# A two-block transformer kernel: input transposed on the host and normalised after the first projections, gate matmuls in three passes, and weight halves made by casting and accumulating transfers

## The chip, the cores and the metric

One core of one Trainium2 chip runs the whole program. The metric is the time of one execution on the device in microseconds (us), taken as the median over runs; the profile is of one execution.

## The reference

Two blocks work on 256 tokens of width 1024, all in float32. Cut to what matters:

```python
h = rms_norm(x, norm1_g)
proj = h @ w_in
(rx, rgate, q, kc, vc, ks, vs, kw, vw, nsa_g, mg_rnn, mg_attn) = jnp.split(proj, splits, axis=-1)
hr = rg_lru(causal_dwconv(rx, ...), rg_w_a, rg_b_a, rg_w_x, rg_b_x, lru_lambda)   # gates: block-diagonal products
y_rnn = (hr * gelu(rgate)) @ w_rnn_out
o = nsa(q, kc, vc, ks, vs, kw, vw, nsa_g, ...)   # keys and queries are RMS-normalised per head
x = x + (sigmoid(mg_rnn) * y_rnn + sigmoid(mg_attn) * (o @ w_attn_out)) @ w_out
up = causal_dwconv(rms_norm(x, norm2_g) @ w_up, ...)
x = x + (gelu(gate) * val) @ w_down
# second block: mixer of attention and gated MLP, layer norms, SwiGLU
```

## The kernel before

**Precision.** Nearly every product is made of three passes in fp32r, a rounded 32-bit form. A weight chunk w is split into a high part WH = round(w), which ScalarE (ACT) writes by a copy (L630), and a low part WL = w − WH, which VectorE (DVE) writes (L1075). Activations are split likewise (BH and BL, CH and CL, AH and AL, kept side by side in BHL, CHL, AHL). TensorE (PE) adds high×high, low×high and high×low in PSUM. `f_tile` is the form with weights stationary: for each of two column halves, 16 matmuls on WH (L1736, L1737), a wait for the low part, then 8 on WL (L1741).

**Chunks.** The weights come as a stream of 135 chunks, most of 128×2048 floats (1 MB), in one order that every engine's program follows. SyncE's queue (SP) loads chunk after chunk into RAW slots (two through most of the program); a slot is loaded anew when its last chunk's low part has been written. WH and WL have three slots; chunk c's are free when PE is through chunk c−3. In iteration c of its loop ACT (and DVE behind it) does `split(c + 2)`, reads the results of chunk c out of PSUM (`side(c)`), and does the attention work that falls into this window (`window(c - W0)`). Each engine works strictly in its written order; semaphores do the rest.

The chunks up to the end of the attention stage, by number: 0 to 3 kv (keys and values), 4 and 5 cmp, 6 to 9 q, 10 and 11 w1 (fp32, not split), 12 to 14 rnn, 15 mg0, 16 ri0, 17 and 18 rnn, 19 mg1, 20 ri1, 21 mg2, 22 and 23 rnn, 24 mg3, 25 ri2, 26 mg4, 27 and 28 rnn, 29 mg5, 30 ri3, 31 and 32 rnn, 33 mg6, 34 mg7, 35 ri4, 36 to 39 ao. An rnn chunk projects the recurrent branch, mg a merge gate, ri the recurrent gates of one group of two tiles (three in ri1), ao the attention's output.

**The opening.** x is loaded in token order; ACT and DVE sum squares, POOL (GpSimd) takes the root; PE runs 14 fill matmuls meanwhile (L2334), then transposes the scaled first token tile (L2340) and the second against a scaled diagonal (L2345). ACT and DVE evict these with the gain as BH and BL, and kv0 and kv1 start, 48 matmuls of 512 columns (L2018, L2021, L2024).

**The attention stage.** It begins in chunk 17 and has 12 units spread over windows. PE computes scores (L1859); DVE masks and reduces (L1096, L1098); ACT takes exponentials (L651); DVE scales; PE transposes (L1870); ACT copies half of the transposed tile PT (L663), DVE the other half (L1120); PE multiplies with the values (L1893). The ri chunks use fp32 matmuls straight from the convolved XC (L2070), with 42-row cross blocks where a block straddles two tiles (L2078, L2080); ACT reads them with tanh (L807, L808). Two PSUM banks serve cmp, rnn, mg and ri in turn: matmul group m waits until group m−2 has been read. One to three chunks after an ri chunk ACT's window holds its exponential and tanh, and the "root stage": square root (L726) and gelu (L728), each with a table load.

Of the kernel before, what the change touches and what calls it, by code (L numbers as in the profile page):

```python
# [23 lines left out]
ACT = mybir.ActivationFunctionType  # L24
# [3 lines left out]
P = 128  # L28
TOK = 256
# [41 lines left out]
def gate_cols(g):  # L71

    return RG_TILES[g] * RP + HB
# [17 lines left out]
def chunk_list():  # L91

    out = [("kv", i, CHUNK, True) for i in range(4)]
    out += [("cmp", i, CHUNK, True) for i in range(2)]
    out += [("q", i, CHUNK, True) for i in range(4)]
# [3 lines left out]
    for g in range(NG):  # L99
# [4 lines left out]
        out += [("ri", g, 2 * gate_cols(g), False)]  # L104
# [12 lines left out]
def ffn_order(up, n, down, lag=5):  # L117

    out, d = [], 0
    for i in range(n):  # L120
        out.append((up, i, CHUNK, True))
        if i >= 2 * d + lag:
# [13 lines left out]
               max(RNN_NO[i] for i in range(RG_AT[g], RG_AT[g + 1])) + 1 for g in range(NG)]  # L136
SPLIT_NO = [sum(1 for x in CHUNKS[:c] if x[3]) for c in range(NCH)]
PLAIN = [c for c in range(NCH) if not CHUNKS[c][3]]

# [4 lines left out]
def arrival_slots():  # L144

    last, uses, out = [None] * (NRAW + 3), [0] * (NRAW + 3), {}
    for c, (kind, i, _, is_split) in enumerate(CHUNKS):
# [7 lines left out]
        last[slot] = SPLIT_NO[c]  # L155
# [23 lines left out]
SPLIT_AHEAD = AT[("ri", 0)]  # L179

# [65 lines left out]
def two_block_program(nc, A_w, A_x, A_cols, A_consts, A_g1, A_g2, A_og, A_gln, A_ln1, A_ln2, A_ws, A_out):  # L246
    ctx = ExitStack()
    with ctx:
# [45 lines left out]
        def const(name):  # L294
# [69 lines left out]
        G1 = put("G1", [P, KD], at=pr + 43008)  # L364
# [58 lines left out]
        w_hi, w_lo, chunk_done, tile0_done, ri_part, y_gain, x_again, const_in, g1_in = (sem(n) for n in (  # L423
            "w_hi", "w_lo", "chunk_done", "tile0_done", "ri_part", "y_gain", "x_again", "const_in", "g1_in"))
        warm_ready, rows_in, w0_half, dg_ready, w0_in, ws_in, out_done, act_own, dve_own = (sem(n) for n in (
            "warm_ready", "rows_in", "w0_half", "dg_ready", "w0_in", "ws_in", "out_done", "act_own", "dve_own"))
        pool_own, x_sq, x_rstd, w0_lo, xt_done, xt_hi, xt_lo, k_sq, k_ss = (sem(n) for n in (
            "pool_own", "x_sq", "x_rstd", "w0_lo", "xt_done", "xt_hi", "xt_lo", "k_sq", "k_ss"))
        k_rstd, kn_ready, kt_done, kt_copied, gk_ready, mb_act, mb_dve, gate_tanh = (sem(n) for n in (
            "k_rstd", "kn_ready", "kt_done", "kt_copied", "gk_ready", "mb_act", "mb_dve", "gate_tanh"))  # L430
        gate_ready, q_sq, q_ss, rq_ready, lam_exp, lam_abs, c4_ready = (sem(n) for n in (
            "gate_ready", "q_sq", "q_ss", "rq_ready", "lam_exp", "lam_abs", "c4_ready"))
# [6 lines left out]
        pt0_copied, pt1_copied, pv_done, o_hi, o_lo, rnn_g, la_ready = (sem(n) for n in (  # L439
            "pt0_copied", "pt1_copied", "pv_done", "o_hi", "o_lo", "rnn_g", "la_ready"))  # L440
# [14 lines left out]
        y_mean, y_std, eps_ready, x0_low, y_ln, xt4_done, xt4_hi, xt4_lo, up2_silu, up2_prod = (sem(n) for n in (  # L455
            "y_mean", "y_std", "eps_ready", "x0_low", "y_ln", "xt4_done", "xt4_hi", "xt4_lo", "up2_silu", "up2_prod"))
        up2_hi, up2_lo, z_gain, wt_ready, rnn_in, xw_ready, gate_t_done, x_sq2 = (sem(n) for n in (
            "up2_hi", "up2_lo", "z_gain", "wt_ready", "rnn_in", "xw_ready", "gate_t_done", "x_sq2"))
        half_copied, halves_summed = sem("half_copied"), sem("halves_summed")
# [2066 lines left out]
```

## Time and profile before

| | us |
|---|---|
| median of 3 runs | 811.58 (811.54 to 811.63) |
| the profiled execution's own time | 811.55 |
| its span, first to last instruction | 809.8 |
| PE busy | 799.9 |
| DVE busy | 599.0 |
| ACT busy | 486.6 |
| POOL busy | 27.1 |

The span is what the profile covers; 1.75 us of the execution's time lie around it. Busy time says how long an engine had an instruction in work, with overlapping matmuls counted once; the waits say who held whom. The mean granted clock of TensorE is 0.997.

### The profile page before, as it was taken

How to read it: one execution, taken by the hardware profiler on the slowest of the kernel's cores; microseconds unless marked ns; L12 is line 12 of the kernel's file. 1: busy time of each engine (PE TensorE's matmuls, PEld its weight loads, DVE VectorE, ACT ScalarE, POOL GpSimd, SP SyncE). 2: the span in 40 equal slices, each digit the busy share in tenths (PEclk: the TensorE clock that was granted, in tenths of full speed). 3: DMA queues.
4: the chain of work that ended last, by engine and by line, in shares of the span. 5: the costliest groups of instructions: out<-in, count | busy, mean ns of one | idle time of the engine just before them, and what ended most of it. 6: DMA issues, size and time to landing. Idle time of an engine off the chain costs nothing.

```text
span 809.8 us, 11913 instructions
## 1 busy us (share of the span) xinstructions
PE 799.9 (99%) x4813; PEld 694.6 (86%) x4813; DVE 599.0 (74%) x773; ACT 486.6 (60%) x738; POOL 27.1 (3%) x38
## 2 busy tenths in 40 slices
PE   9999999999999999999999999999999999999996
PEld 8889998888888888988888888888888888888885
DVE  6774698998958986897878678877777665655556
ACT  6555598877767454665666566546755654544552
POOL 1102000000000000000000000020110000000000
PEclk9999999999999999999999999999999999999998
DMA  8446433342434774456555555664453655465431
GB/s 338 160 159 251 169 126 105 118 155 70 154 119 159 251 266 156 156 197 219 161 204 182 197 193 183 253 240 142 144 197 123 211 198 201 170 220 190 162 151 52
DMA packets 22630, 143.79 MB, mean 178 GB/s; under 512 B 2608, under 2 KB 3248, under 8 KB 8240
## 3 DMA queue, kind: packets, MB, share of 16 engines
q1 hardware_dynamic: 20880, 137.72, 48.0%
q10 hardware_dynamic: 1696, 5.31, 1.9%
q8 instruction: 38, 0.62, 0.3%
q14 instruction: 16, 0.13, 0.1%
HBM read 141.97 MB, written 1.05 MB: 177 GB/s over the span
## 4 chain that ended last, share of the span: by engine, by line
PE 92%; ACT 3%; DVE 3%; issue 1%; DMA 1%; DVEq 0%; SPq 0%; ACTq 0%
PE PS L1749 19%; PE PS L1753 10%; PE PS L1802 10%; PE PS L1803 10%; PE PS L1806 10%; PE PS L1736 5%; PE PS L1737 4%; PE PS L1741 4%; PE PS L2120 2%; PE PS L1765 2%; PE PS L2099 2%; PE PS L1859 1%; PE PS L2124 1%; PE PS L1893 1%; PE PS L1870 1%; PE PS L1773 1%
## 5 line engine op out<-in xcount | busy, mean ns | idle before, releaser
L1075 DVE TENSOR_TENSOR WL<-RAW,WH 128x2048 fp32r<-128x2048 f32 (+2 forms) x127 | 284.6, 2242 | 32.3 <-ACT WH L630 32.1
L630 ACT ACTIVATE WH<-RAW 128x2048 fp32r<-128x2048 f32 (+2 forms) x127 | 238.1, 1877 | 51.3 <-PE PS L1806 26.4
L1491 DVE TENSOR_TENSOR HLS<-PS,HLS 128x512 f32<-128x512 f32 x46 | 31.7, 689 | 92.7 <-ACT HLS L978 92.7
L1749 PE MATMUL PS<-CHL,WH 128*128 128x512 f32 x352 | 87.9, 392 | 0.0
L1736 PE MATMUL PS<-BHL,WH 128*126 128x256 f32 (+1 forms) x336 | 83.8, 287 | 0.0
L978 ACT ACTIVATE HLS<-PS 128x512 f32<-128x512 f32 x46 | 27.4, 595 | 90.8 <-PE PS L1753 86.4
L1737 PE MATMUL PS<-BHL,WH 128*126 128x256 f32 (+1 forms) x336 | 81.8, 282 | 0.0
L1749 PE MATMUL PS<-BHL,WH 128*128 128x512 f32 x320 | 79.9, 392 | 0.0
L1749 PEld LDWEIGHTS PS<-CHL,WH 128*128 128x128 f32 x352 | 63.9, 189 | 11.8
L1803 PE MATMUL PS<-WH,AHL 128*128 128x512 f32 x176 | 68.8, 391 | 0.0
L1802 PE MATMUL PS<-WH,AHL 128*128 128x512 f32 x176 | 68.7, 390 | 0.0
L1736 PEld LDWEIGHTS PS<-BHL,WH 128*126 128x126 f32 (+1 forms) x336 | 63.4, 189 | 4.6 <-issue 4.0
L1749 PEld LDWEIGHTS PS<-BHL,WH 128*128 128x128 f32 x320 | 58.1, 189 | 10.7
L1737 PEld LDWEIGHTS PS<-BHL,WH 128*126 128x126 f32 (+1 forms) x336 | 63.5, 189 | 0.0
L1802 PE MATMUL PS<-WH,BHL 128*128 128x512 f32 x160 | 63.2, 395 | 0.0
L1803 PE MATMUL PS<-WH,BHL 128*128 128x512 f32 x160 | 62.4, 390 | 0.0
L1806 PE MATMUL PS<-WL,AHL 128*128 128x512 f32 x176 | 54.4, 390 | 0.0
L1753 PEld LDWEIGHTS PS<-CHL,WL 128*128 128x128 f32 x352 | 48.0, 190 | 3.4
L1753 PE MATMUL PS<-CHL,WL 128*128 128x256 f32 x352 | 49.1, 282 | 0.0
L1741 PE MATMUL PS<-BHL,WL 128*126 128x256 f32 (+1 forms) x336 | 46.7, 281 | 0.0
L1753 PEld LDWEIGHTS PS<-BHL,WL 128*128 128x128 f32 x320 | 43.7, 190 | 3.1
L1502 DVE SCALAR_TENSOR_TENSOR CG<-HLS,CV,CG 128x255 f32<-128x255 f32 (+1 forms) x96 | 44.1, 481 | 1.7
(313 smaller groups left out, 1312.3 us busy)
## 6 DMA issues: line engine op xcount, KB each, us to landing
RAW<-in_w_stream SPq DMA_DIRECT2D x108, 1024.0 KB, 4.9
RAW<-in_w_stream SPq DMA_DIRECT2D x11, 1008.0 KB, 4.8
RAW<-in_w_stream SPq DMA_DIRECT2D x8, 704.0 KB, 4.7
WF<-in_w_stream SPq DMA_DIRECT2D x2, 1024.0 KB, 5.2
LN<-in_ln ACTq DMA_DIRECT2D x2, 1024.0 KB, 5.1
WF<-in_w_stream SPq DMA_DIRECT2D x4, 294.0 KB, 3.6
X<-in_x SPq DMA_DIRECT2D x2, 512.0 KB, 4.2
RAW<-in_w_stream SPq DMA_DIRECT2D x2, 512.0 KB, 6.6
```

Of the source, the lines that this page charges most:

```text
L630: eng.activation(WH[:, c % NSLOT, 0:CHUNKS[c][2]], raw(c), ACT.Copy).then_inc(w_hi, 1)
L1075: eng.tensor_tensor(WL[:, c % NSLOT, 0:CHUNKS[c][2]], raw(c), f32(WH[:, c % NSLOT, 0:CHUNKS[c][2]]), ALU.subtract).then_inc(w_lo, 1)
L1491: eng.tensor_tensor(HLS[:, n % 4, :, :], PS[:, bank:bank + 2, 0:TOK], HLS[:, n % 4, :, :], ALU.add)\
L1502: ins = eng.scalar_tensor_tensor(o, HLS[:, i % 4, v, 0:TOK - s], col("fw", (2 - s) * 2 * N_UP + f), o, ALU.mult, ALU.add)
L1736: eng.matmul(out, wh, H[0:parts, k, :], start=(k == 0), stop=False)
L1737: eng.matmul(out, wh, L[0:parts, k, :], start=False, stop=False)
L1741: last = eng.matmul(out, wl, H[0:parts, k, :], start=False, stop=(k == nk - 1))
L1749: eng.matmul(PS[:, bank, :], wh, HL[:, k, :, :].rearrange("p a t -> p (a t)"), start=(k == 0), stop=False)
L1753: last = eng.matmul(PS[:, bank, 0:TOK], wl, HL[:, k, 0, :], start=False, stop=(k == KD - 1))
L1802: eng.matmul(out, H[:, k, tile], wh, start=(start and n == 0), stop=False)
L1803: eng.matmul(out, L[:, k, tile], wh, start=False, stop=False)
L1806: last = eng.matmul(out, H[:, k, tile], WL[:, s, lo_:lo_ + cols], start=False, stop=(stop and n == len(ks) - 1))
```

## The change

- **Opening.** The host also passes x transposed, with the gain in front (`xt`, tile XTG with XT inside it). CH and CL are XT times the gain, split, without the row's root. kv0 to kv3 and q are computed from CH and CL, eight pieces of kv0 and kv1 at a time (`first_high`, `first_low`), and the row scale rsx is applied where V, the keys' and the queries' squares and roots are made. x itself is loaded behind kv3. After kv3 PE spreads the row scales by two fp32 matmuls, DVE scales XT (`input_normed`), and ACT and DVE split it into BH and BL for the rest. q0 and q1 come before cmp. 11 fills stand in place of 14.
- **Gates.** The ri chunks are split as others are; ACT rounds XC into AH (`rg_round`), DVE writes the remainder into AL, and each product has three passes. A cross block is 106 columns wide with zeros, to start at the bank's partition 0.
- **Casting transfers.** For the 16 split chunks from 17 to 39 that are not mg (`CAST`), WH is written by a transfer on POOL's queue, which reads the chunk again and rounds it. RAW is still loaded for the low part, which DVE now writes in iteration c−1.
- **Accumulating transfers.** For mg1 to mg7 (`ADDED`), ACT still writes WH. At the end of iteration c−2 it writes −w, rounded, into WL (`negated`), and a transfer on POOL's queue adds the chunk from memory in place. The RAW slot is free after the negation.
- **PT.** ACT copies both halves at once.
- Some semaphores are joined, without another order.

```diff
+ADDED = [AT[("mg", i)] for i in range(1, 8)]
+CAST = [c for c in range(AT[("ri", 0)] + 1, AT[("ao", 3)] + 1) if CHUNKS[c][3] and c not in ADDED]
...
+            for c in range(NCH):
+                if c + 2 in CAST:
+                    s, n = (c + 2) % NSLOT, CAST.index(c + 2)
+                    source = A_w[OFFS[c + 2]:OFFS[c + 3]].rearrange("(p n) -> p n", p=P)
+                    eng.wait_ge(chunk_done, c)
+                    if n >= 2:
+                        eng.wait_ge(wh_in[n % 2], 16 * (n // 2))
+                    eng.dma_start(WH[:, s, 0:CHUNKS[c + 2][2]], source).then_inc(wh_in[n % 2], 16)
+                if c + 2 in ADDED:
+                    s, n = (c + 2) % NSLOT, ADDED.index(c + 2)
+                    source = A_w[OFFS[c + 2]:OFFS[c + 3]].rearrange("(p n) -> p n", p=P)
+                    eng.wait_ge(neg_ready, n + 1)
+                    if n:
+                        eng.wait_ge(wl_in, 16 * n)
+                    eng.dma_start(WL[:, s, 0:CHUNKS[c + 2][2]], source, accum_op=ALU.add).then_inc(wl_in, 16)
...
+            def negated(c):
+                eng.activation(WL[:, c % NSLOT, 0:CHUNKS[c][2]], raw(c), ACT.Copy, scale=-1.0).then_inc(neg_ready, 1)
...
+            def rg_round(i):
+                G, t = RG_OF[i]
+                eng.wait_ge(mb_dve, RNN_NO[i] + 1)
+                eng.activation(AH[0:RP, i, :], XC[:, G % 2, t, :], ACT.Copy).then_inc(xc_hi, 1)
...
                 if c >= W0:
                     window(c - W0)
+                if c + 2 in ADDED:
+                    negated(c + 2)
...
-                if c and CHUNKS[c - 1][0] == "ri" and c - 1 != SPLIT_AHEAD or c == UNIT_FIRST:
+                if c + 1 in CAST:
                     split(c + 1)
+                if c + 1 < NCH and CHUNKS[c + 1][0] == "ri":
+                    s, n = (c + 1) % NSLOT, CHUNKS[c + 1][2]
+                    wait_both(eng, c + 1)
+                    eng.tensor_tensor(WL[:, s, 0:n], raw(c + 1), f32(WH[:, s, 0:n]), ALU.subtract).then_inc(rg_low, 1)
...
                 if CHUNKS[c][3]:
                     slot, before, _ = ARRIVAL[c]
                     if before is not None:
-                        eng.wait_ge(w_lo, before + 1)
+                        if before in ADDED:
+                            eng.wait_ge(neg_ready, ADDED.index(before) + 1)
+                        elif CHUNKS[before][0] == "ri":
+                            eng.wait_ge(rg_low, RG_LOW_NO[CHUNKS[before][:2]])
+                        else:
+                            eng.wait_ge(w_lo, LOW_NO[before] + 1)
...
-            def f_tile(out, c, col0, m, H, L, nk=KD, parts=P):
+            def f_tile(out, c, col0, m, H, L, nk=KD, parts=P, first_use=False):
...
                     eng.matmul(out, wh, H[0:parts, k, :], start=(k == 0), stop=False)
                     eng.matmul(out, wh, L[0:parts, k, :], start=False, stop=False)
-                eng.wait_ge(w_lo, SPLIT_NO[c] + 1)
+                wait_low(eng, c)
...
                         for which in range(2):
-                            last = eng.matmul(PS[0:RP, banks[t], 256 * which:256 * which + 256],
-                                              w[0:RP, which, RP * t:RP * t + RP], XC[:, i % 2, t, :], start=(which == 0),
+                            rows = wh[0:RP, which, RP * t:RP * t + RP]
+                            eng.matmul(outs[which], rows, AH[0:RP, k, :], start=(which == 0), stop=False, skip_group_check=True)
+                            eng.matmul(outs[which], rows, AL[0:RP, k, :], start=False, stop=False, skip_group_check=True)
+                        for which in range(2):
+                            last = eng.matmul(outs[which], wl[0:RP, which, RP * t:RP * t + RP], AH[0:RP, k, :], start=False,
                                               stop=(t == 2), skip_group_check=True)
...
-            for _ in range(14):
+            for _ in range(11):
                 eng.matmul(PS[:, 4, 0:P], WARM[:, :], WARM[:, :], start=True, stop=True)
-            eng.wait_ge(g1_in, 32)
-            for kp in range(4):
-                eng.wait_ge((x0_low, dg_ready)[kp // 2], 1)
...
```

How instructions moved, at three places. First PE at the start of the program. Before (WARM is the fill tile, CN holds the identity, XN the scaled x, DG the diagonal):

```order
L2334 MATMUL PS<-WARM 128x128 x13
L2340 MATMUL PS<-CN,XN 128x128 [waits x0_low,g1_in]
L2340 MATMUL PS<-CN,XN 128x128
L2340 MATMUL PS<-CN,XN 128x128 [waits x0_low]
L2340 MATMUL PS<-CN,XN 128x128
L2340 MATMUL PS<-CN,XN 128x128 [waits dg_ready]
...
L2345 MATMUL PS<-DG,X_115 128x128 [waits dg_ready]
L2345 MATMUL PS<-DG,X_115 128x128 x7
L2018 MATMUL PS<-WH,BHL 128x512 [waits xt_hi,w0_half]
L2018 MATMUL PS<-WH,BHL 128x512 x3
```

Now:

```order
L2504 MATMUL PS<-WARM 128x128 x10
L2183 MATMUL PS<-WH,CHL 128x512 [waits xt_ready,w_part_hi]
L2183 MATMUL PS<-WH,CHL 128x512
L2186 MATMUL PS<-WL,CHL 128x512 [waits w_part_lo]
L2186 MATMUL PS<-WL,CHL 128x512
L2189 MATMUL PS<-WH,CHL 128x512 [waits xt_lo]
L2189 MATMUL PS<-WH,CHL 128x512
```

The transposes are gone, and the first weight matmuls stand right behind the fills, two for each pass instead of four.

Second ACT in iteration 17, the one in which chunk 19 (mg1) is prepared; its exponential and tanh (AA, TR), then the root stage of group 0. Before:

```order
L718 ACTIVATE AA<-TR 126x512 [waits la_ready]
L719 ACTIVATE TR<-TR 126x512 [waits act_own]
L721 ACTIVATE XC<-AA 126x512 [waits ix_ready]
L726 ACT_TABLE_LOAD
L726 ACTIVATE XC<-TR 126x512 [waits w_ready]
L728 ACT_TABLE_LOAD
L728 ACTIVATE RGT<-RGT 126x512 [waits rnn_g]
L794 ACTIVATE XC<-PS,CV 126x256 [waits chunk_done]
```

Now:

```order
L808 ACTIVATE AA<-TR 126x512 [waits la_ready]
L809 ACTIVATE TR<-TR 126x512 [waits act_own]
L811 ACTIVATE XC<-AA 126x512 [waits ix_ready]
L816 ACT_TABLE_LOAD
L816 ACTIVATE XC<-TR 126x512 [waits w_ready]
L818 ACT_TABLE_LOAD
L818 ACTIVATE RGT<-RGT 126x512 [waits rnn_g]
L715 ACTIVATE WL<-RAW 128x2048
L747 ACTIVATE AHL<-XC 126x256 [waits mb_dve]
L892 ACTIVATE XC<-PS,CV 126x256 [waits chunk_done]
```

The negation (WL<-RAW) and the rounding of the convolved tile stand between the root stage and the next chunk's results.

Third POOL's queue, behind the compressed keys' root (crs). Before:

```order
L575 TENSOR_SCALAR tmp<-css 64x1 [waits kc_sq]
L576 TENSOR_TENSOR crs<-tmp,half 64x1 [waits pool_own]
L597 TENSOR_TENSOR rs_87<-ss1s,half 128x1 [waits x1_ss] x2
L601 TENSOR_TENSOR RQK<-RT 128x512 [waits rope_parts] x2
L604 AFFINE_SELECT WS<-WS 128x1024 [waits ws_in]
```

Now (17 more transfers follow in the same manner until rs_87):

```order
L634 TENSOR_SCALAR tmp<-css 64x1 [waits kc_sq]
L635 TENSOR_TENSOR crs<-tmp,half 64x1 [waits pool_own]
L669 DMA WH<-in_w_stream 128x2016 [waits chunk_done] x2
L676 DMA WL<-in_w_stream 128x2048 [waits neg_ready]
L669 DMA WH<-in_w_stream 128x968 [waits wh_in0,chunk_done]
L676 DMA WL<-in_w_stream 128x2048 [waits wl_in,neg_ready]
L669 DMA WH<-in_w_stream 128x2016 [waits wh_in1,chunk_done]
```

The queue that did nothing in the attention stage now issues 23 transfers in it, each casting one behind the accumulating ones of earlier chunks.

## Rows read from the trace of the kernel before

**Rows 1.** The page: span, and busy us (share of the span) with instructions.
```profile
span 809.8 us, 11913 instructions
...
PE 799.9 (99%) x4813; PEld 694.6 (86%) x4813; DVE 599.0 (74%) x773; ACT 486.6 (60%) x738; POOL 27.1 (3%) x38
```
**Rows 2.** Waits of PE: engine, line, who was waited for; us, times, longest.
```profile
PE PS L1870 <- DVE PT L1120: 0.8, 1, 0.8
```
**Rows 3.** Timeline of the opening: start us, us, engine, line, operation.
```profile
1.10 6.08 PE L2334 MATMUL PS<-WARM 128*128 128x128 f32 x28 [1.10 <-DVE WARM L1641]
...
4.56 0.63 ACT L1024 ACTIVATE XN<-X 128x512 f32<-128x512 f32 x1 [1.57 <-DMA X<-in_x]
...
7.42 1.06 PE L2340 MATMUL PS<-CN,XN 128*128 128x128 f32 x8 [0.24 <-ACT XN L1027]
...
10.12 1.18 PE L2018 MATMUL PS<-WH,BHL 128*128 128x512 f32 x4
...
11.64 1.92 ACT L630 ACTIVATE WH<-RAW 128x2048 fp32r<-128x2048 f32 x1
...
21.14 0.39 PE L1802 MATMUL PS<-WH,BHL 128*128 128x512 f32 x1
```
**Rows 4.** Busy us by stretch: PE, PEld, DVE, ACT, POOL, PEclk, DMA share, GB/s.
```profile
10.10:21.30 11.20, 11.20 (x52) 9.28 (x51) 10.60 (x19) 9.10 (x12) 0.00 (x0) 1.00 0.89 352
98.60:137.10 38.50, 38.44 (x297) 33.32 (x294) 33.98 (x47) 34.20 (x70) 0.00 (x0) 1.00 0.36 124
```
**Rows 5.** DMA issues: count, KB each, median us from issue to landing.
```profile
RAW<-in_w_stream SPq DMA_DIRECT2D x108, 1024.0 KB, 4.9
...
CN<-in_consts SPq DMA_DIRECT2D x1, 229.0 KB, 8.8
```
**Rows 6.** PE timeline of chunk 16 (ri0) and the scores behind it.
```profile
98.89 1.89 PE L2070 MATMUL PS<-XC,WF 126*126 126x256 f32 x8
100.71 0.41 PE L2078 MATMUL PS<-XC,WF 42*42 42x256 f32 x1
...
101.70 1.14 PE L1859 MATMUL PS<-KT,QT 64*128 64x256 f32 x8
```
**Rows 7.** ACT timeline, iterations 17 to 20.
```profile
105.22 1.90 ACT L630 ACTIVATE WH<-RAW 128x2048 fp32r<-128x2048 f32 x1
...
115.59 0.63 ACT L728 ACTIVATE RGT<-RGT 126x512 f32<-126x512 f32 x1
...
122.85 0.62 ACT L663 ACTIVATE PT<-PS 128x512 f32<-128x512 f32 x1
123.57 0.47 ACT L807 ACTIVATE TR<-PS,hba 126x256 f32<-126x256 f32 x1
```
**Rows 8.** PE timeline: first low pass of chunk 19 (mg1); chunk 20 (ri1).
```profile
117.80 1.12 PE L1741 MATMUL PS<-BHL,WL 128*128 128x256 f32 x8
...
122.51 3.08 PE L2070 MATMUL PS<-XC,WF 126*126 126x256 f32 x12
```
**Rows 9.** DVE timeline in window 4.
```profile
101.53 2.25 DVE L1075 TENSOR_TENSOR WL<-RAW,WH 128x2016 fp32r<-128x2016 f32 x1
```
**Rows 10.** ACT's root stages and PE's low passes of chunks 24, 29 and 34.
```profile
148.68 0.85 ACT L728 ACTIVATE RGT<-RGT 126x768 f32<-126x768 f32 x1
...
152.61 1.12 PE L1741 MATMUL PS<-BHL,WL 128*128 128x256 f32 x8
...
188.10 0.63 ACT L728 ACTIVATE RGT<-RGT 126x512 f32<-126x512 f32 x1
...
195.22 1.12 PE L1741 MATMUL PS<-BHL,WL 128*128 128x256 f32 x8
...
227.70 0.63 ACT L728 ACTIVATE RGT<-RGT 126x512 f32<-126x512 f32 x1
...
232.58 1.12 PE L1741 MATMUL PS<-BHL,WL 128*128 128x256 f32 x8
```
**Rows 11.** Busy us by stretch at the end, columns as in rows 4.
```profile
802.70:805.40 2.70, 0.00 (x0) 0.00 (x0) 2.59 (x5) 1.53 (x3) 0.00 (x0) 1.00 0.13 48
805.60:809.80 4.20, 0.00 (x0) 0.00 (x0) 1.68 (x5) 0.00 (x0) 0.00 (x0) 0.50 0.50 187
```

More of the change, by code:

```diff
@@ L71, in gate_cols @@
 def gate_cols(g):
[L73 removed]
+    return RG_TILES[g] * RP + 64 + HB
 def rnn_rows(g):
@@ L154, in arrival_slots @@
         out[c] = (slot, last[slot], uses[slot])
-        last[slot] = SPLIT_NO[c]
+        last[slot] = c
         uses[slot] += 1
@@ L1026, in _ @@
-            eng.wait_ge(x_rstd, 1)
-            eng.activation(XN[:, 0, 0:512], X0[:, 0, 0:512], ACT.Copy, scale=rsx[:, 0:1]).then_inc(x0_low, 1)
-            eng.wait_ge(g1_in, 32)
-            for kp, ready in enumerate((w0_half, w_hi)):
-                eng.wait_ge((w0_in, raw_in[ARRIVAL[0][0]])[kp], 16)
-                part = slice(CHUNK // 2 * kp, CHUNK // 2 * kp + CHUNK // 2)
-                eng.activation(WH[:, 0, part], raw(0)[:, part], ACT.Copy).then_inc(ready, 1)
-                gained_hi(kp)
@@ L1233, in side @@
-                if kind == "kv" and i == 0:
+                if kind == "kv" and i == 1:
+                    key_sums(0)
+                if kind == "q" and i == 0:
                     eng.wait_ge(const_in, 32)
@@ L1691, in _ @@
                     rg_squares(rg_group(c - W0, RG_SQUARES))
-                if CHUNKS[c][:2] not in SUMS_FIRST and kind != "ri" and c != W0 and c + 1 != UNIT_FIRST or c == SPLIT_AHEAD:
+                if c == 1:
+                    x_squares()
+                if c == 3:
+                    input_normed()
+                if kind == "w1" and i == 0:
+                    queries_normed(1, 0)
+                if c == 4:
+                    key_sums(1)
+                    for kp in range(4):
+                        eng.wait_ge(xt_hi, KD - 1 + kp + 1)
+                        pair = slice(2 * kp, 2 * kp + 2)
+                        eng.tensor_tensor(BL[:, pair, :], XT[:, pair, :], f32(BH[:, pair, :]), ALU.subtract).then_inc(xt_lo, 1)
+                if c == 5:
+                    query_sums(0)
+                    keys_normed(0)
+                if CHUNKS[c][:2] not in SUMS_FIRST and c + 2 not in CAST and c != W0:
                     split(c + 2)
@@ L1704, in _ @@
                     rg_scan(G)
+                if c == 1:
+                    roots_diagonal()
+                if c == 5:
+                    keys_normed(1)
+                if kind == "w1" and i == 0:
+                    queries_normed(1, 1)
+                if c == W0:
+                    decay_rates()
                 side(c)
```

526 lines of the change are left out of this document (306 added, 220 removed).

## Prediction

> **What bounds it now.** I read the page first: TensorE (PE) is busy 799.9 us of an 809.8 us span [rows 1]. Overlapping matmuls flatter that number, so I asked who TensorE waits for. After the opening one wait is listed, 0.8 us for a copy on VectorE [rows 2]. In the attention stage the matmuls start at their usual cadence with no hole: PE's instruction stream is the time, and whatever stops it is paid in full. The exception is the opening: fill matmuls start at 1.10, transposes of the normalised input at 7.42, and the first weight matmul at 10.12 [rows 3]. The span is 809.8, the execution's time 811.55, 0.03 below the median, 811.58; I sum against 811.55.
>
> **The opening.** The three steps before the matmuls (squares, scaled copies, transposes) leave the path: 24 transposing instructions, 7.42 to 10.12. The remaining limit is the 11 fills. 28 starts took 6.08 less a tail [rows 3], so 22 end near 1.10 + 22 × 0.21 = 5.8. The first pieces (256 KB of weights and 266 KB of input) equal the 512 KB that the first squaring waited for until 4.56 [rows 3]; with a copy of a quarter chunk (a quarter of 1.92 us) they are ready at about 5.1. The same 48 matmuls ran from 10.12 to 21.14, 0.227 each; from 5.8 they end at 16.7: −4.4. Behind them stands the supply. Chunks kv0, kv1, kv2 and the transposed input are 4.2 MB; at 352 GB/s [rows 4] from about 3.1 (the 512 KB transfer's landing less its 1.5 us) the last lands at 15.1; its high copy takes 1.92 [rows 3] to 17.0 (+0.3), its low part another 2.25 [rows 9] to 19.3, where PE wants it eight matmuls after 17.0, at 18.8 (+0.5). The matmuls that spread the row scales, two fp32 ones of two instructions at some 0.11, add 0.4. Net **−3.2**, from −4.4 (supply no limit) to 0 (the queue that now also carries the input and x feeds PE late).
>
> **The gates.** Before, a group of two 126-row tiles issues 8 instructions in 1.89, 0.22 each, then four pairs of 42-row matmuls from 100.71 to 101.70, 0.25 a pair [rows 6]; over five groups that is 44 and 20. Now 66 matmuls in three passes at 0.12 (eight low-part matmuls take 1.12 with their tail [rows 8]) replace the 44: 7.8 for 9.5. The cross blocks become 30 pairs. If a pair still runs together, they cost 3.5 for 4.5; if one after the other, 7.1. I take together, since K = 64 matmuls on separate row halves do so before (8 in 1.14 [rows 6]). Net **−2.7**, up to +0.9. The work added on ACT and DVE (rounding and remainder of 11 tiles of 256 columns, each no longer than the 512-column copy of 0.62 [rows 7]) lies beside matmuls; without that cover its 22 pieces would cost up to 14.
>
> **Relief of ACT and DVE.** 16 high copies of up to 1.9 leave ACT for transfers on POOL's queue; DVE loses seven low parts of 2.25 [rows 9], and its half of twelve PT copies goes to ACT. PE waited for them only 0.8 [rows 2]: **−0.8**. The sixteen casting transfers have a whole chunk or more of PE time, so I cost them at nothing; they double the reading of those chunks.
>
> **What replaces the low part of a merge gate.** The new chain is: ACT writes −w (one copy, 1.9), POOL's queue wakes, 1 MB is read and added in place, and only then may PE start the low pass. ACT's copy stands at the end of iteration c−2, behind everything there. The chunks, by iteration:
> - mg1 (chunk 19, ACT iteration 17). Before, ACT runs without a hole from 105.22 (the high copy of mg1) to 116.22 (the gelu of group 0): 26 rows, none with an idle time ahead, the first and last in [rows 7]. The negation follows. PE starts mg1's low pass at 117.80 [rows 8]. Moreover the high copy of mg1 needs its RAW slot, whose last reader is now DVE's low part of chunk 17. That part stands one chunk later than before, where DVE ran another at 101.53 to 103.78 [rows 9]; with 4.9 us of transfer [rows 5] the data lands at 108.7, 3.5 after 105.22. SP's queue and the exponentials of unit 0 stand behind it. The negation so ends at 116.2 + 3.5 + 1.9 = 121.6.
> - ri1 (chunk 20). The negation of mg2 is put before the gates' tanh. PE's third tile waits for that tanh: two tiles done at 122.7 + 1.4 = 124.1, while ACT comes free of its PT copy at 123.5 [rows 7], now 0.4 later since it does both halves (an estimate from its 0.62 for one), then 1.9 of negation and two tanh of 0.47: 126.7. **+2.6**. The transfer of mg2 then lies beside it.
> - mg3, mg5, mg7 (chunks 24, 29, 34). Their negation stands behind the same root stage, which ends at 149.53, 188.73 and 228.33; the low passes start at 152.61, 195.22 and 232.58 [rows 10]. With transfer time T the stalls are T − 1.2, T − 4.6, T − 2.3.
> - mg4 and mg6 have no root stage ahead; nothing.
>
> No row shows an accumulating transfer. The nearest is a plain 1 MB load, 4.9 us, as the lower end; the upper is 8.8, a transfer that lands behind others [rows 5]. In two of three cases another 1 MB load starts with it, since the negation frees a RAW slot. I take **T = 5.5**, near the plain row, because the DMA engines are busy only 0.36 of the time here [rows 4]. Then: mg1 121.6 + 5.5 − 117.8 = **+9.3**, ri1 +2.6, mg3 **+4.3**, mg5 **+0.9**, mg7 **+3.2**.
>
> The Trainium skill (DMA: Bandwidth & Descriptors, "Anatomy of one DMA — SWDGE (gpsimd) path") gives for a transfer issued by GpSimd about 2.0 us plus bytes at 436 GB/s, some 4.4 us for this megabyte. By that estimate the stalls would be 1.1 shorter each; no run here shows one, and the sum keeps to the row of 4.9 and above.
>
> **The clock.** The fills start every 0.21 us, the 128-column transposes after them (8 in 1.06) about every 0.11 [rows 3]: PE is at 1.2 GHz at first and at 2.4 after 6 us of work. After PE's last matmul (before 802.7) the granted clock is 0.50 from 805.6 on [rows 11]. So a stall of some 3 us or more may be followed by half rate, which costs at most half of 6 us each. I take **+1** over all, since two stalls are that long. The skill (TensorE: Matmul & The Clock Gate, "HAM oscillation — how this bites in real kernels") tells the same of kernels that wait for DMA; what it adds is the rival below.
>
> **Sum.** −3.2 − 2.7 − 0.8 = −6.7; + 9.3 + 2.6 + 4.3 + 0.9 + 3.2 + 1.0 = +21.3. 811.55 + 14.6 = **826**.
>
> **Rivals.**
> - *The negations run ahead, and only the gains are left*: 811.55 − 6.7 = **805**. For it: ACT is free of 16 copies. Against it: those copies don't stand between 105.22 and 116.22, nor in the root stages, and even a transfer of no length leaves mg1 at 118.1 for 117.8. It needs mg1's negation to end before 112.3 (with T = 5.5). 12 in 100.
> - *Short waits*: raw data of mg1 in time and T = 4.9. Then mg1 116.2 + 1.9 + 4.9 − 117.8 = 5.2, ri1 2.6, mg3 3.7, mg5 0.3, mg7 2.6: 14.4 − 6.7, **819**. 22 in 100.
> - *The clock falls at each long stall* (mg1, mg3, mg7): 3 × 3 in place of 1: **834**. 12 in 100.
> - *The accumulating transfer is slow*, 8.8: each of four stalls 3.3 longer: **839** and more. 3 in 100.
> - *Even*: gains and stalls of 7 cancel, **811.5**, if mg1 alone stalls. 5 in 100.
> - My forecast: 46 in 100.
>
> **Numbers.** Within 0.2% (1.6 us) I call it no change, about what three runs of this kernel can tell. Slower holds 83 in 100, the same 5, faster 12. The range takes in the forecast, the short waits and the clock: 813 to 840.
>
> **What would show it.** After: the first weight matmul near 5.8 and the 48 done near 17; gate groups about 0.5 us shorter. In the waits of PE, the DMA of WL as releaser in mg1's low pass, of 6 us or more, and again in mg3 and mg7; ACT's TI ahead of the third tile of ri1. The casting transfers should appear in no wait. I am wrong in size if T is far from 5.5, wrong in kind if PE waits for no WL transfer, and wrong in the opening if PE then waits for high copies of chunks kv2 or later by more than 1 us.

## The result and the profile after

The changed kernel takes **865.25 us** (median of 4 runs, 864.2 to 867.74) against 811.56 for the kernel before beside it: 1.0667 of its time, interval 1.0652 to 1.0681. Slower, as forecast, but by 53.7 us where 14.6 were forecast; the range ended at 840.

The page of the changed kernel, answering to [rows 1], [rows 5] and, by PEclk, [rows 4]:

```profile
span 866.0 us, 12016 instructions
...
PE 811.4 (94%) x4829; PEld 707.0 (82%) x4829; DVE 592.0 (68%) x788; ACT 490.5 (57%) x752; POOL 54.1 (6%) x69
...
PEclk9999968968999899999999999999999999999998
...
RAW<-in_w_stream SPq DMA_DIRECT2D x107, 1024.0 KB, 5.0
...
WH<-in_w_stream POOLq DMA_DIRECT2D x8, 1008.0 KB, 12.2
WL<-in_w_stream POOLq DMA_DIRECT2D x7, 1024.0 KB, 10.4
...
WH<-in_w_stream POOLq DMA_DIRECT2D x4, 1024.0 KB, 7.0
```

PE, busy 99% of its span before, is now busy 94%, and its clock is cut in slices of the attention stage; the last slice reads 8 as it did before. The accumulating transfer takes 10.4 us from issue to landing, not 5.5. The waits of PE, answering to [rows 2] (engine, line, releaser; us, times, longest):

```profile
PE PS L1906 <- DMA WL<-in_w_stream: 38.5, 7, 10.4
...
PE PS L1901 <- DVE XC L1422: 2.8, 1, 2.8
```

All seven merge gates wait for their low weights, not four (line L1906 is their low pass, L1901 their first high pass). PE's timeline of the opening, answering to [rows 3]:

```profile
1.11 4.40 PE L2504 MATMUL PS<-WARM 128*128 128x128 f32 x22 [1.11 <-DVE yeps L1785]
5.61 0.70 PE L2183 MATMUL PS<-WH,CHL 128*128 128x512 f32 x2
...
16.86 0.62 PE L2189 MATMUL PS<-WH,CHL 128*128 128x512 f32 x2
17.31 0.39 PE L1967 MATMUL PS<-WH,CHL 128*128 128x512 f32 x1
```

The weights start at 5.61 and the 48 matmuls are through at 17.31, 3.8 earlier than before; no wait for a high copy of kv2 or later is among PE's waits. The gates of chunk 16 (ri0), answering to [rows 6]:

```profile
95.46 0.36 PE L2238 MATMUL PS<-AHL,WH 126*126 126x256 f32 x1
...
97.05 0.37 PE L2250 MATMUL PS<-AHL,WH 42*106 42x256 f32 x1
97.06 0.36 PE L2252 MATMUL PS<-AHL,WH 42*106 42x256 f32 x1
...
97.84 1.03 PE L2024 MATMUL PS<-KT,QT 64*128 64x256 f32 x8
```

They take 2.38 us for 2.81. Each pair of 42-row matmuls still starts together.

The chain of mg1: ACT, answering to [rows 7] (the high copy, the gelu, the negation), then POOL's queue:

```profile
105.39 1.92 ACT L712 ACTIVATE WH<-RAW 128x2048 fp32r<-128x2048 f32 x1 [3.84 <-DMA RAW<-in_w_stream]
...
115.78 0.63 ACT L818 ACTIVATE RGT<-RGT 126x512 f32<-126x512 f32 x1
116.31 1.89 ACT L715 ACTIVATE WL<-RAW 128x2048 fp32r<-128x2048 f32 x1
```

```profile
118.51 0.90 POOL L676 DMA_DIRECT2D WL<-in_w_stream  x1 [22.38 <-ACT WL L715]
119.09 0.88 POOL L669 DMA_DIRECT2D WH<-in_w_stream  x1
```

PE at the low passes of mg1 (two rows), mg3, mg5 and mg7, answering to [rows 8] and [rows 10]:

```profile
128.99 2.08 PE L1906 MATMUL PS<-BHL,WL 128*128 128x256 f32 x8 [10.40 <-DMA WL<-in_w_stream]
134.27 1.16 PE L1906 MATMUL PS<-BHL,WL 128*128 128x256 f32 x8
...
182.63 0.58 PE L1906 MATMUL PS<-BHL,WL 128*128 128x256 f32 x1 [9.34 <-DMA WL<-in_w_stream]
...
240.66 0.58 PE L1906 MATMUL PS<-BHL,WL 128*128 128x256 f32 x1 [3.92 <-DMA WL<-in_w_stream]
...
287.36 0.58 PE L1906 MATMUL PS<-BHL,WL 128*128 128x256 f32 x1 [5.76 <-DMA WL<-in_w_stream]
```

Eight low matmuls took 2.08 behind the wait and 1.16 five microseconds later: the first ran at half rate, which is 1.2 GHz for 2.4. The stretches (columns as in [rows 4]) say so as well:

```profile
118.50:129.00 10.50, 0.10 (x2) 0.01 (x1) 5.72 (x10) 6.36 (x14) 1.46 (x2) 0.50 0.93 233
129.00:135.00 6.00, 6.00 (x30) 6.00 (x31) 4.69 (x7) 0.29 (x2) 0.00 (x0) 0.55 0.51 170
```

While PE waits, the DMA engines are busy 93% of the time for 233 GB/s. The opening of [rows 4] had 89% and 352 GB/s: the same engine time moves over a third less.

### The profile page after: what moved, and what is told of

Read it like the earlier page. It is cut to its first block, busy times and chain, and to the rows that moved or that the text cites. A ratio compares the mean times of both kernels' runs of the same rounds, so it can differ in the third digit from the quotient of the medians.

```text
span 866.0 us, 12016 instructions
## 1 busy us (share of the span) xinstructions
PE 811.4 (94%) x4829; PEld 707.0 (82%) x4829; DVE 592.0 (68%) x788; ACT 490.5 (57%) x752; POOL 54.1 (6%) x69
## 4 chain that ended last, share of the span: by engine, by line
PE 76%; issue 11%; DMA 9%; ACT 2%; DVE 1%; POOL 0%; DVEq 0%; SPq 0%; POOLq 0%; ACTq 0%
PE PS L1914 18%; PE PS L1918 9%; PE PS L1967 9%; PE PS L1968 9%; PE PS L1971 9%; DMA WL<-in_w_stream 8%; PE PS L2291 2%; PE PS L1906 2%; PE PS L1901 2%; PE PS L1930 2%; PE PS L1902 2%; PE PS L2271 2%; PE PS L2295 1%; PE PS L1938 1%; PE PS L2277 1%
## 5 line engine op out<-in xcount | busy, mean ns | idle before, releaser
L1191 DVE TENSOR_TENSOR WL<-RAW,WH 128x2048 fp32r<-128x2048 f32 (+2 forms) x119 | 266.4, 2238 | 39.4 <-ACT WH L712 27.2
L712 ACT ACTIVATE WH<-RAW 128x2048 fp32r<-128x2048 f32 (+3 forms) x115 | 214.1, 1864 | 58.1 <-DMA RAW<-in_w_stream 25.4
L1901 PE MATMUL PS<-BHL,WH 128*126 128x256 f32 (+1 forms) x336 | 91.4, 305 | 2.9 <-DVE XC L1422 2.8
L1902 PE MATMUL PS<-BHL,WH 128*126 128x256 f32 (+1 forms) x336 | 89.1, 299 | 0.0
L1906 PE MATMUL PS<-BHL,WL 128*126 128x256 f32 (+1 forms) x336 | 52.1, 301 | 38.5 <-DMA WL<-in_w_stream 38.5
L1906 PEld LDWEIGHTS PS<-BHL,WL 128*126 128x126 f32 (+1 forms) x336 | 47.2, 208 | 40.0 <-DMA WL<-in_w_stream 40.0
L1901 PEld LDWEIGHTS PS<-BHL,WH 128*126 128x126 f32 (+1 forms) x336 | 69.5, 207 | 7.9 <-issue 7.7
L1902 PEld LDWEIGHTS PS<-BHL,WH 128*126 128x126 f32 (+1 forms) x336 | 69.5, 207 | 0.0
L1918 PE MATMUL PS<-BHL,WL 128*128 128x256 f32 x320 | 44.6, 282 | 0.0
## 6 DMA issues: line engine op xcount, KB each, us to landing
WH<-in_w_stream POOLq DMA_DIRECT2D x8, 1008.0 KB, 12.2
WL<-in_w_stream POOLq DMA_DIRECT2D x7, 1024.0 KB, 10.4
```

The costliest lines, as they stand in the source:

```text
L712: eng.activation(WH[:, c % NSLOT, 0:CHUNKS[c][2]], raw(c), ACT.Copy).then_inc(w_hi, 1)
L1191: eng.tensor_tensor(WL[:, c % NSLOT, 0:CHUNKS[c][2]], raw(c), f32(WH[:, c % NSLOT, 0:CHUNKS[c][2]]), ALU.subtract).then_inc(w_lo, 1)
L1901: eng.matmul(out, wh, H[0:parts, k, :], start=(k == 0), stop=False)
L1902: eng.matmul(out, wh, L[0:parts, k, :], start=False, stop=False)
L1906: last = eng.matmul(out, wl, H[0:parts, k, :], start=False, stop=(k == nk - 1))
L1918: last = eng.matmul(PS[:, bank, 0:TOK], wl, HL[:, k, 0, :], start=False, stop=(k == KD - 1))
```

## The experiments

Fourteen kernels ran. Unless said otherwise each edit is made to the changed kernel.

### Which part costs: neither list, then one of them

`neither` has both lists empty; `no_added` keeps the casting transfers of the same 16 chunks and lets ScalarE and VectorE split mg1 to mg7; `no_cast` keeps the accumulating ones.

```diff
-ADDED = [AT[("mg", i)] for i in range(1, 8)]
+ADDED = []                      # neither, no_added
-CAST = [c for c in range(AT[("ri", 0)] + 1, AT[("ao", 3)] + 1) if CHUNKS[c][3] and c not in ADDED]
+CAST = []                       # neither, no_cast
```

> The changed kernel with both lists of transfers empty: ScalarE writes every high part, VectorE every low part; the new opening, the three-pass gates and the joined PT copy stay. Theory (the whole loss is in the transfers of the merge gates' low weights and in the clock that falls behind them): the stalls of TensorE on WL and the half rate go, and what is left is the opening (first low pass behind the opening 3.35 us earlier in the changed kernel's trace, 3.77 by the second merge gate) and up to 2.3 for the four further gate groups: 806, between 804.5 and 808. Rival (the gates in three passes or ScalarE's joined PT copy cost something that the stalls hide): 811 or more. Mean granted clock back at 0.99 or above.

> The changed kernel without the accumulating transfers: the low parts of mg1 to mg7 are written by VectorE again, ScalarE still writes their high parts, and the 16 casting transfers stay. Theory: a casting transfer alone lands in about 5.1 us (two such issues in the changed kernel's trace) and has a chunk or more of TensorE time, so this is equal to the kernel without both lists, 806, within 1. Rival (the casting transfers cost by themselves, by landing late or by taking the queue of the raw loads): slower than the kernel without both lists by 2 us or more, with WH from a transfer among TensorE's or VectorE's waits.

> The changed kernel without the casting transfers: ScalarE writes those 16 high parts again, the accumulating transfers stay and are alone on GpSimd's queue. Theory (the accumulation itself makes most of the 10.4 us; the one issue in the changed kernel's trace with no casting transfer behind it took 8.3): 8 to 9 us from issue to landing, each of seven stalls some 2 us shorter, and the clock falls at fewer of them: 848, between 840 and 858. Rival (the casting transfer behind it is what makes it slow): 5 to 6 us, and 830 or less.

Measured: neither **817.93** (ratio 1.008, 1.0067 to 1.0094), no_added **812.04** (1.0007, 0.9998 to 1.0015), no_cast **863.97** (1.0639, 1.0621 to 1.0656). Three readings. First, the accumulating transfers, with all that hangs on them, carry the loss: 865.25 − 812.04 = 53.2. Second, both first expectations (806) missed: without any accumulation the kernel is no faster than the one before. The gains that I had put at 6.7 are gone. Third, the casting transfers are not free, they *help*: 5.9 us between the two kernels. That holds for these two kernels; beside accumulating transfers the help is gone: the changed kernel takes 1.3 us more than no_cast, with intervals that overlap. In `neither`, PE waits for ACT's exponentials, which stand behind high copies:

```profile
PE PS L2024 <- ACT SM L736: 5.2, 2, 4.4
PE PS L2238 <- issue: 2.3, 1, 2.3
```

The second row is ri1 waiting for its low part and for the remainder of XC, which VectorE wrote until 121.2.

In no_cast the accumulating transfer is alone on its queue, and my theory of 8 to 9 us fell, and its rival of 5 to 6 too:

```profile
L676 POOL DMA_DIRECT2D WL<-in_w_stream x7: 866/868/1072, 114.7 to 271.4; - x7
...
DMA to landing us min/median/max: 9.9/10.4/11.9
```

The median is 10.4 with and without a casting transfer issued behind it on the same queue, so that isn't what makes it slow. The 8.3 that my expectation went by belongs to mg6, where the raw load that starts with the transfer has 358 KB in place of 1 MB:

```profile
WL<-in_w_stream POOLq DMA_DIRECT2D x1, 1024.0 KB, 8.3
RAW<-in_w_stream SPq DMA_DIRECT2D x1, 358.0 KB, 3.0
```

### When the negation is written

```diff
                 eng.activation(WH[:, c % NSLOT, 0:CHUNKS[c][2]], raw(c), ACT.Copy).then_inc(w_hi, 1)
+                if c in ADDED:
+                    negated(c)
...
-                if c + 2 in ADDED:
-                    negated(c + 2)
```

> The changed kernel with the negation right behind the high copy of the same chunk instead of at the end of the iteration; both kinds of transfer stay. The accumulating transfer then starts 8 to 15 us earlier. Theory (the stalls are late start plus a transfer of 10.4): mg2, mg4, mg5, mg6 and mg7 stall no more, mg3 some 4, mg1 about 1 behind a bank wait of some 5, little half rate: 819, between 813 and 826. Rival (the transfer takes longer the more it overlaps other transfers, so an early start is lost again): above 835, with 12 us or more from issue to landing.

Measured: **822.27** (1.0134, 1.012 to 1.0148), PE's waits for WL 38.5 to 4.9 with T hardly changed (8.5 to 11.5, median 9.9). The theory of a late start held: 43 of 53 us come back by moving one instruction of the loop. PE's longest waits are now in mg3 (4.6 for WL) and at mg1's bank (3.5 for DVE's XC), as expected; five of 0.5 to 1.0 lie beside them.

### What T is made of

Three kernels, one run each (the kernel before took 811.57 beside them), so their times count only to a few us. The first leaves out the addition, so that WL holds the whole weight in place of its low part; the second holds the raw load back until the transfer has landed; the third adds only half of the columns.

```diff
-                    eng.dma_start(WL[:, s, 0:CHUNKS[c + 2][2]], source, accum_op=ALU.add).then_inc(wl_in, 16)
+                    eng.dma_start(WL[:, s, 0:CHUNKS[c + 2][2]], source).then_inc(wl_in, 16)                  # plain_add
+                    eng.dma_start(WL[:, s, 0:CHUNK // 2], source[:, 0:CHUNK // 2], accum_op=ALU.add)...      # half_add
...
-                            eng.wait_ge(neg_ready, ADDED.index(before) + 1)
+                            eng.wait_ge(wl_in, 16 * ADDED.index(before) + 16)                                # hold_raw, on SP
```

> The changed kernel with the same seven transfers into WL, but without adding: each overwrites WL with the chunk, so the low part of the merge gates' weights is left out. Theory (from shares of the engines in the traces so far: an accumulating megabyte takes the 16 DMA engines 5.3 us of their time, a plain or casting one 2.9; T = a fixed 2.1, plus this, plus the engine time of the raw load beside it, 2.9): T falls from 10.4 to 8, and the time to about 845. Rival (GpSimd's queue is slow whatever it does): T stays above 9.5 and the time above 858.

> The changed kernel in which the raw load that the negation frees is held back until the accumulating transfer of the same chunk has landed, so that the two no longer share the DMA engines. Theory (shared engine time): T falls from 10.4 to about 7.4. Stalls 3 us shorter each would give 845, unless the raw loads come late and the high copies behind them with it. Rival (the accumulation is slow by itself and the raw load doesn't matter): T stays at 10.

> The changed kernel in which the accumulating transfer covers only the first 1024 of the 2048 columns (the rest of WL keeps the negated high part, so part of the sum is left out). Theory: 2.1 fixed, half of 5.3, and 2.9 of the raw load beside it: T 7.7 in place of 10.4, time about 845. Rival (a fixed cost of accumulating, or of waking the queue): T above 9.

Measured: plain_add 843.84 us, hold_raw 856.14, half_add 848.55. The time from issue to landing (min, median, max of the seven), first plain_add, then hold_raw, then half_add:

```profile
DMA to landing us min/median/max: 5.3/7.1/7.4
```

```profile
DMA to landing us min/median/max: 7.9/8.0/8.4
```

```profile
DMA to landing us min/median/max: 7.4/7.8/8.1
```

All three theories held in kind. A megabyte by this queue without adding takes 5.3 when only a small raw load lies beside it (one transfer, that of mg6) and 7.1 beside a full one; with adding 8.0 with no raw load beside it and 10.4 beside a full one. So T = 10.4 is 5.3, plus 2.7 for adding, plus 2.4 for the raw load that the negation itself sets off. The engine time agrees. The queue's rows (packets, MB, share of 16 engines), first no_cast, where only the accumulating transfers use it, then no_added, where only the casting ones do:

```profile
q0 software_dynamic: 1008, 7.34, 4.3%
```

```profile
q1 hardware_dynamic: 21312, 138.64, 48.9%
q0 software_dynamic: 2304, 14.05, 5.1%
```

Over spans of 861.8 and 810.2 us that is 37.1 us for 7.34 MB, 5.0 per MB, against 2.9 for casting and 2.9 for plain loads. Adding costs the DMA engines 1.7 times as much, and holding the raw load back trades that for a raw load which is late: ACT's high copies wait 42.4 us for raw data in hold_raw and 25.4 in the changed kernel. It won 9 us, not the 20 expected.

By the fit of the Trainium skill (DMA: Bandwidth & Descriptors, "Anatomy of one DMA — SWDGE (gpsimd) path") the estimate for this megabyte was about 4.4 us. A casting transfer that ran with nothing beside it came near it (5.1). The accumulating ones took 8.0 even without a raw load beside them; there the two differ, and the measurement decides.

The time goes with T: from plain_add to half_add 4.7 us for 0.7, from there to the changed kernel 16.7 for 2.6. That is 6.5 us for each us of T between 7.1 and 10.4, from single runs. T stands in front of seven low passes, of which four waited at 7.1, six at 7.8 and all seven at 10.4, so that below 7.1 the slope is likely less; no run has such a T.

### The clock

```diff
                 s = c % NSLOT
+                for _ in range(REPEATS.get(c, 0) if col0 == 0 else 0):      # 5, 1, 4, 2, 2, 1, 3 for mg1 to mg7
+                    for k in range(nk):
+                        wh = WH[0:parts, s, col0 + k * m:col0 + k * m + m]
+                        eng.matmul(out, wh, H[0:parts, k, :], start=(k == 0), stop=False)
+                        eng.matmul(out, wh, L[0:parts, k, :], start=False, stop=(k == nk - 1))
```

> The changed kernel in which TensorE fills its stalls with work: before the first high pass of each of mg1 to mg7 it computes that pass 5, 1, 4, 2, 2, 1 and 3 times more (1.9 us each, overwritten by the pass that counts), so that it is busy while WL is late. The transfers are untouched and T stays 10.4. Theory (of the 54 us that the change costs over the kernel without accumulation about 14 are half rate behind stalls, from 60.4 us of growth over the attention stage less 48 of stalls plus some 2 of gate matmuls saved): 851, between 847 and 856, with a mean granted clock at or above 0.98. Rival (the rate costs little, the rest is waiting): 862 or more.

Measured: **864.51** (1.0648, 1.063 to 1.0666), mean granted clock 0.985 for 0.964. My theory of 14 us fell, and the time is the rival's: 0.7 us below the changed kernel, no more than the runs scatter. The half rate is real: from the first to the second low pass of a merge gate PE took 12.5 us more than before, over the seven (mg1: 134.27 − 128.99 = 5.28 for 2.88), and 4.2 more with the repeats. The first low pass of mg1, which took 2.08 there, takes 1.22 here:

```profile
130.36 1.22 PE L1912 MATMUL PS<-BHL,WL 128*128 128x256 f32 x8 [1.83 <-DMA WL<-in_w_stream]
```

But what PE wins behind one stall it waits for at the next, because the next transfer starts when ACT has negated, and ACT's root stage moved little: of the 8.3 us won between low passes only 2.0 show in the issue of the last of the seven transfers, at 277.0 in the changed kernel and at 275.0 here. Its landing is what the end hangs on. Here it landed 10.3 us later, at 285.3, and the repeats ran past it: the low pass of mg7 began at 288.43, without a wait. So 3.1 us that had been won were spent on repeats. T itself was longer, 11.0 in the median for 10.4, with the low pass of mg1 at 130.36 for 128.99; why, no run here tells. By an estimate from these rows (0.7 + 3.1) the clock costs some 4 us, and more if T had stayed at 10.4; its share of the 53 us stays open.

```profile
L677 POOL DMA_DIRECT2D WL<-in_w_stream x7: 855/865/898, 119.0 to 275.0; - x7
...
DMA to landing us min/median/max: 10.1/11.0/11.4
```

### Where the opening's gain went

`old_gates_cast` is no_added with the gate products of before; `old_gates` has no casting transfers either, so it is the kernel before with the new opening and the joined PT copy. The diff shows the main places.

```diff
-        out += [("ri", g, 2 * gate_cols(g), True)]
+        out += [("ri", g, 2 * gate_cols(g), False)]
...
-                            eng.matmul(outs[which], rows, AH[0:RP, k, :], start=(which == 0), stop=False, skip_group_check=True)
...
+                            last = eng.matmul(outs[which], w[0:RP, which, RP * t:RP * t + RP], XC[:, i % 2, t, :], start=(which == 0),
+                                              stop=(t == 2), skip_group_check=True)
```

> The kernel of no_added with the gate products of before: the ri chunks in fp32 from the convolved XC, 42-row cross blocks, no rounding of XC on ScalarE and no remainder on VectorE; new opening, casting transfers (12 chunks, ri not among them) and joined PT copy stay. In no_added TensorE waited 1.1 and 0.8 in ri1 for low parts and for ScalarE, and 3.0 at mg1's bank. Theory (the opening's 3.8 is lost where VectorE and ScalarE lag, partly by the rounding): without the rounding those waits shrink, but the five groups take 2.4 us more of TensorE's time; 811, between 809.5 and 812.5. Rival (rounding costs nothing): 814 or more.

> The kernel before with the new opening and ScalarE's joined PT copy alone: old gates, no transfers on GpSimd's queue. Theory (the wait of 6 us in neither's seventh window, where unit scores wait for a PSUM bank that ScalarE reads late, comes from ScalarE's load: joined PT copies and high copies): the rounding is gone but the PT copies stay, so part of it remains: 813, between 810 and 816. Rival (the opening's gain comes through when the rounding is gone): 808 or less.

Measured: old_gates_cast **811.07** (0.9995, 0.9987 to 1.0004), old_gates **813.27** (1.0015, 1.0006 to 1.0024; its runs fell in two groups, near 811.7 and near 813.3, and the profiled one is of the first). Both theories held. The opening, 3.4 us ahead at the second chunk of rnn, ends where the kernel before ends or behind it, and for another reason in each of the two. In old_gates PE waits for ACT's exponentials, as in `neither`, since no transfer takes high copies off ACT:

```profile
PE PS L2013 <- ACT SM L736: 3.9, 3, 2.7
```

In old_gates_cast that wait is gone, and ACT's timeline shows what takes the lead instead:

```profile
105.27 1.92 ACT L713 ACTIVATE WH<-RAW 128x2048 fp32r<-128x2048 f32 x1 [3.35 <-DMA RAW<-in_w_stream]
```

The high copy of mg1 stood at 105.22 before [rows 7] and stands at 105.27 now. ACT idles 3.35 us for the raw data, because chunk 17's slot comes free one iteration later than before; in old_gates, which casts nothing, the same copy starts at 101.87 without a wait. PE is early and waits at mg1's bank (2.3 for DVE's XC) and in ri1. That points to a one-chunk edit of old_gates_cast, `cast_from_18`. `halves_again` is the same with the second half of PT copied by DVE again, as before:

```diff
-CAST = [c for c in range(AT[("ri", 0)] + 1, AT[("ao", 3)] + 1) if CHUNKS[c][3] and c not in MERGE]
+CAST = [c for c in range(AT[("ri", 0)] + 2, AT[("ao", 3)] + 1) if CHUNKS[c][3] and c not in MERGE]
```

> The kernel of old_gates_cast (new opening, old gates, casting transfers, no accumulation) with chunk 17 taken off the list of casting transfers, so that ScalarE writes its high part and VectorE its low part one iteration earlier. In old_gates_cast mg1's raw load started at the same time as before the change and ScalarE idled 3.35 us for it, because it takes the slot of chunk 17, whose low part stood later. Theory (that is where the opening's 3.4 us are lost: 2.5 of TensorE's wait at mg1's bank and 1.5 in ri1): both shrink, 809, between 808 and 810.5. Rival (VectorE is the limit there whatever frees the slot): 811, and TensorE still waits 2 us or more at mg1's bank.

> The same with the PT copies shared again: ScalarE copies one half (0.62 instead of 1.05), VectorE the other. Theory (the third tile of ri1 waits for ScalarE, which has the joined copy ahead of its tanh): another 0.4 off each wait for ScalarE behind a PT copy, 0.5 to 1 us in all below the kernel with the joined copy. Rival (VectorE is the busier engine and hands the 0.6 back): equal or slower.

Measured: cast_from_18 **808.46** (0.9967, 0.9954 to 0.9979), halves_again **808.9** (0.9968, 0.9956 to 0.998). The theory held for the slot: the same copy now starts at 101.72 without a wait, and PE's waits at mg1 and in ri1 shrink to 0.3 and 0.5.

```profile
101.72 1.90 ACT L713 ACTIVATE WH<-RAW 128x2048 fp32r<-128x2048 f32 x1
```

```profile
PE PS L2227 <- ACT TI L907: 0.5, 1, 0.5
PE PS L1891 <- DVE XC L1421: 0.3, 1, 0.3
```

This kernel beats both, by 3.0 us the one before and by 56.8 the changed one. So the opening pays when ACT is relieved and mg1's slot isn't held, and neither alone was enough. Sharing PT again gave nothing that shows (0.4 us the other way, within the scatter): the wait for ACT's TI is gone, one of 0.8 for DVE's half of PT, that of [rows 2], is back.

### The gates alone, and the whole change with its starts mended

`gates_from_18` is cast_from_18 with the three-pass gates; `neg_first_18` is neg_first with chunk 17 off the casting list, by the same edit of CAST.

> The kernel of cast_from_18 with the three-pass gates of the change (so: the change without accumulating transfers and without the cast of chunk 17). Theory (the gate products save TensorE time, 2.7 us in the prediction, and what the rounding adds on ScalarE and VectorE costs waits in ri1): in the traces with the new gates TensorE gained 0.4 over each two-tile group and 1.2 over the three-tile one, and waited 2.0 in ri1; against the 808.46 of cast_from_18 this gives 2.4 less and some 1.5 more: 807.5, between 806 and 809. Rival (the rounding stands in the way of more than it saves, as no_added's 812.04 beside old_gates_cast's 811.07): 809.3 or more.

> The whole change, accumulating transfers included, with two moves: the negation right behind the high copy, and chunk 17 off the casting list, so that mg1's raw load starts some 6 us earlier. In neg_first TensorE waited 4.6 for WL in mg3, 3.5 at mg1's bank and 0.3 elsewhere. Theory: mg3's wait stays, most of mg1's goes: 822.27 less 3 to 6, 818, between 815 and 820. Rival (the accumulating transfers cost by the traffic that they add, wherever they start): 821 or more.

Measured: gates_from_18 **810.63** (0.9991, 0.9982 to 1.0), neg_first_18 **819.22** (1.0091, 1.0076 to 1.0107). The gates cost 2.2 us here, and my theory of a gain fell; with chunk 17 on the list they cost 1.0 (812.04 for 811.07). Their five ri chunks are also cast, which the old gates don't need, and that was not taken apart. PE's waits in gates_from_18:

```profile
PE PS L1902 <- DVE XC L1423: 2.2, 1, 2.2
...
PE PS L2239 <- ACT TI L907: 0.7, 1, 0.7
PE PS L2239 <- issue: 0.4, 1, 0.4
```

The first is mg1's bank again: the wait of 0.3 has become 2.2, and DVE had idled 1.92 us for the casting transfer of chunk 18, which took 7.7 us with a raw load ahead of it; in cast_from_18 the same transfer, issued at the same time, took 5.8, and DVE's low part behind it started at 101.78 in place of 103.21. Whether the gates or this meeting of two transfers is to blame for it was not separated. The second kernel came out as its theory had it. What is left of the accumulation's cost is mostly waiting: it lies 8.6 us above gates_from_18, and PE waits 6.9 us for WL, 4.6 of them in mg3.

## Why the prediction was wrong in size

The sign was right and so was the mechanism, ACT's negation, POOL's queue, a transfer, and PE behind it; the sizes were not. The forecast lay 39.2 below the time. Two steps failed.

**T, the accumulating transfer, "T = 5.5, near the plain row, because the DMA engines are busy only 0.36 of the time here".** It measured 10.4. The plain row lacked the 2.7 for adding, and the busy share of the stage said nothing of the moment: the raw load that the negation frees starts 0.3 us ahead of the transfer, each time (1 MB in six of the seven). I had named that load and given it no price. At 6.5 us per us of T the 4.9 missing would be 32 us; 21.4 of them are measured, from T = 7.1 up, and the rest is an extrapolation to 5.5. The four stalls came out as 10.4, 9.3, 3.9 and 5.8 for 9.3, 4.3, 0.9 and 3.2.

With it fell **"mg4 and mg6 have no root stage ahead; nothing"** and mg2's transfer "beside" ri1: they waited 4.8, 2.2 and 2.1 (mg4, mg6, mg2). No root stage stands ahead of them, but the negation stands last in its iteration all the same, and 10.4 us is more than PE's time from there. With T = 5.5 they would have been close to nothing. My upper bound of 8.8 was itself too low.

**The gains, "−3.2 − 2.7 − 0.8 = −6.7".** The accumulation apart they came to +0.5 (no_added, where DVE keeps the seven low parts), a miss of 7.2. The *opening* was sized well: first weight at 5.61 for 5.8, through at 17.31 for “near 17”, 3.4 us ahead at the next stages. But I put a gain at the start of a chain into the sum without asking what else keeps its old date. The raw load of mg1 did, which I had even listed as late (I had it land at 108.7; it landed at 105.4, which is why the negation ended at 118.2 and not at 121.6). I had charged it to the negation alone, not to mg1's high copy and so to the opening. In old_gates, which casts nothing, the lead went into 3.9 us of waiting for ACT's exponentials. The *gates* take 0.43 less in a group, for 0.54 forecast, but **"the work added on ACT and DVE … lies beside matmuls"** does not hold in iterations 17 to 20: in `neither`, ri1 waits 2.3 for the remainder of XC, and in no_added 1.0 and 0.7. Net the gates cost 2.2 with chunk 17 off the list and 1.0 with it on. (Two slips in my sums change little: twenty pairs at 0.25 are 5.0, not 4.5, and in the opening 48 matmuls from 10.12 to 21.14 are 0.230 each, not 0.227.) The *relief* of ACT is worth more than 0.8: 5.9 with the new gates, the difference of `neither` and no_added, and 2.2 with the old ones (old_gates and old_gates_cast). But it only pays for load on ACT that I had counted at nothing: without transfers the new gates cost 4.7 (817.93 in `neither`, 813.27 in old_gates), and PE waits for the exponentials.

Together 32 + 7 = 39, the whole miss. That it comes out so well is in part luck, since the slope below 7.1 was not measured. Read from the trace the same miss has these parts: waits for WL 38.5 for 17.7 (20.8 more), half rate behind them 12.5 in the merge gates for 1 (11.5 more), the gains 7.2, and ri1 0.4 less.

**ri1's third tile** waited 2.2 for ACT's TI, 2.6 forecast. **The casting transfers** appear in no wait of PE, as forecast, though they land 12.2 us after issue in the changed kernel; they stand behind the accumulating ones. **The clock**, put at 1 by "two stalls are that long", fell at every long stall; the matmuls of the merge gates alone lost 12.5 to it, more than the 9 of the rival that had it as its mechanism. What the time pays of that may be less, where a slow stretch is taken out of the next wait: with the waits filled, 0.7 us was won, beside some 3 that the last repeats overshot and a T that was longer. What the clock costs by itself stays open.

## What to carry to other kernels

When an engine's work is replaced by a chain (write, queue, transfer), price the chain from its last link's *issue*, and ask what else the first link releases at the same instant: here it released the load that competed with it. Put the chain's first instruction as soon as its inputs are there, not where the code has room; that was worth 43 us here. And when the start of a program gets faster, follow every buffer's release to the first stage that keeps its old time, for there the gain ends; moving one chunk off a list gave 2.6 us back.

## What the runs showed of the hardware

- An accumulating transfer of 1 MB from memory into SBUF took 8.0 us with no plain load beside it (hold_raw) and 10.4 beside one of 1 MB (changed kernel, no_cast); without adding 5.3 beside one of 358 KB and 7.1 beside one of 1 MB (plain_add). It took 5.0 us of the 16 DMA engines per MB (no_cast), plain and casting transfers 2.9 (no_added).
- GpSimd was occupied 0.87 us by the issue of an accumulating transfer (no_cast) and 0.54 by that of a plain one from the same line (plain_add).
- A casting transfer of 1 MB landed 5.1 us after its issue when nothing was beside it (changed kernel, before 101 us), the plain load on SyncE's queue in 4.9 (kernel before).
- After a stall of 10.4 us the granted clock was 0.55 over the next 6 us. Keeping TensorE busy in the stalls (busy_wait) raised the mean clock from 0.964 to 0.985; the time fell by 0.7 us of 865, within the scatter, with 3 us of overshoot in it.
